# Reordering the first stage of a two-layer trunk kernel: weight units, token load, filler products and row spreading

## What is computed

```python
mod_all = einsum('bd,lde->lbe', silu(c), w_mod) + b_mod      # w_mod: (2, 1024, 6*1024)
shift1, scale1, gate1, shift2, scale2, gate2 = split(mod_all[i], 6)
h = rms_norm(x, norm_g[i, 0]) * (1 + scale1) + shift1
y = pool_mixer(h, pool_w, pool_scale)        # window means, then a 256x256 product per group
x = x + gate1 * rms_norm(y, norm_g[i, 1])
h = rms_norm(x, norm_g[i, 2]) * (1 + scale2) + shift2
y = swiglu(h, ffn_w_gu, ffn_w_down)
```

## Time and profile before

| what | us |
|---|---|
| median of 3 runs | 1280.43 (1277.85 to 1281.45) |
| profiled execution, its own time | 1280.07 |
| its span, first to last instruction | 1278.2 |
| first product of the FFN in it | 70.39 after the span's start |

### The profile page before, as it was taken

One profiled execution on the slowest core, in us unless ns is written; L12 is line 12 of the kernel. 1 busy time (PEld: TensorE's weight loads), 2 busy tenths in 40 slices (PEclk: granted clock), 3 DMA queues, 4 the chain that ended last, 5 costly groups with the idle time before them and its releaser, 6 DMA issues.

```text
span 1278.2 us, 31266 instructions
## 1 busy us (share of the span) xinstructions
PE 1249.0 (98%) x14625; PEld 779.1 (61%) x14625; DVE 387.3 (30%) x591; ACT 214.7 (17%) x320; POOL 109.8 (9%) x134
## 2 busy tenths in 40 slices
PE   6799999999999999999999999999999999999997
PEld 3589999989774354545455454554545545454555
DVE  1567778979872110101101011010101201011012
ACT  3253333474842000000000000000000000000001
POOL 4220000010030000020010010002001000200100
PEclk9899999999999999999999999999999999999999
DMA  9998998959379999999999999999999999999980
GB/s 371 414 358 295 334 333 305 364 197 395 123 245 420 425 423 425 424 402 424 424 407 424 424 409 411 424 409 404 423 421 396 422 424 412 404 424 415 399 355 36
DMA packets 114055, 477.47 MB, mean 374 GB/s; under 512 B 10944, under 2 KB 37280, under 8 KB 113792
## 3 DMA queue, kind: packets, MB, share of 16 engines
q1 hardware_dynamic: 106112, 457.29, 89.1%
q0 software_dynamic: 7664, 17.87, 4.6%
q10 hardware_dynamic: 144, 0.26, 0.1%
HBM read 465.79 MB, written 11.16 MB: 373 GB/s over the span
## 4 chain that ended last, share of the span: by engine, by line
PE 95%; DVE 2%; ACT 1%; POOL 1%; DMA 1%; issue 1%; SPq 0%; DVEq 0%; ACTq 0%
PE ps L2421 23%; PE ps L2407 23%; PE ps L2396 23%; PE ps L1927 7%; PE ps L1928 7%; PE ps L1929 7%; PE ps L1952 1%; PE ps L2014 1%; PE ps L1911 1%; DMA raw<-w_mod 1%; DVE wlo L1572 1%; PE ps L2205 1%; PE ps L1975 0%; PE ps L2035 0%; PE ps L2350 0%
## 5 line engine op out<-in xcount | busy, mean ns | idle before, releaser
L1799 DVE TENSOR_TENSOR act_in<-act_in,ps 128x1344 f32<-128x1344 f32 x16 | 24.9, 1555 | 527.1 <-PE ps L2407 527.1
L1927 PE MATMUL ps<-thi,whi 128*128 128x256 f32 x480 | 136.0, 283 | 0.8 <-DVE wlo L1421 0.8
L1928 PE MATMUL ps<-tlo,whi 128*128 128x256 f32 x480 | 135.8, 283 | 0.0
L1929 PE MATMUL ps<-thi,wlo 128*128 128x256 f32 x480 | 135.8, 283 | 0.0
L2396 PE MATMUL ps<-raw,turned_in 128*32 128x448 f32 x1296 | 123.7, 539 | 0.0
L2407 PE MATMUL ps<-ring_w,turned_in 128*32 128x448 f32 x1248 | 120.6, 539 | 0.0
L2421 PE MATMUL ps<-ring_w,turned_act 128*32 128x256 f32 x2016 | 117.2, 379 | 0.0
L2421 PE MATMUL ps<-raw,turned_act 128*32 128x256 f32 x2016 | 115.5, 379 | 0.0
L1220 ACT ACTIVATE act_in<-ps 128x1344 f32<-128x1344 f32 x16 | 20.7, 1292 | 548.6 <-PE ps L2396 548.6
L1290 DVE TENSOR_TENSOR wlo<-raw,whi 128x2048 fp32r<-128x2048 f32 x41 | 92.9, 2289 | 32.7 <-ACT whi L901 32.7
L2421 PEld LDWEIGHTS ps<-raw,turned_act 128*32 128x32 f32 x2016 | 82.4, 110 | 33.5 <-issue 3.5
(11 more groups left out here) (324 smaller groups left out, 1332.0 us busy)
## 6 DMA issues: line engine op xcount, KB each, us to landing
raw<-moe_w_gu SPq DMA_DIRECT2D x96, 896.0 KB, 12.9
ring_w<-moe_w_gu SPq DMA_DIRECT2D x96, 896.0 KB, 13.0
raw<-w_mod SPq DMA_DIRECT2D x84, 512.0 KB, 5.7
rows<-moe_w_gu SPq DMA_DIRECT2D x48, 896.0 KB
raw<-moe_w_down SPq DMA_DIRECT2D x48, 896.0 KB, 13.9
ring_w<-moe_w_down SPq DMA_DIRECT2D x48, 896.0 KB, 13.4
raw<-ffn_w_gu SPq DMA_DIRECT2D x44, 512.0 KB, 5.6
rows<-moe_w_down SPq DMA_DIRECT2D x24, 896.0 KB
```

What stands on the lines that cost most here:

```text
L1799: dve.tensor_tensor(act_3, act_3, gate_up_ps(1), ALU.mult).then_inc(e_act, 1)
L1927: pe.matmul(out, a_hi, b_hi, start=start, stop=False, skip_group_check=check)
L1928: pe.matmul(out, a_hi, b_lo, start=False, stop=False, skip_group_check=check)
L1929: return pe.matmul(out, a_lo, b_hi, start=False, stop=stop, skip_group_check=check)
```

## The change

It touches the first stage alone:

- **Order of units.** `HEAD` is now group by group: 1, 0, 2, 4, 3. The four shift1 units come ahead of all gate1 units; before, the two groups were interleaved. SP loads in this order, DVE takes all four gate units after the edge columns (before: two ahead of them and two behind), PE's list follows.
- **Tokens first.** `x` (1 MB) is loaded ahead of unit 0; before, it was loaded behind unit 1.
- **Zero products.** 85 at the begin, 8 before the pooled product, 20 before the second mixing product, 20 after each of the first three gate units, 12, 12 and 16 between the waits for the residual, and 20 behind each of units 16, 17 and 18. The tile of zeros is now cleared by DVE.
- **Rows spread with 128 rows of contraction.** The two rows are loaded into row 0 of two tiles of zeros that DVE clears first, so that the product by ones has 128 rows of contraction. POOL waits for the clearing before it issues these loads.
- **PE's order.** The pooled product comes ahead of the spread and of units 2 and 3; units 12 to 15 are spread over the waits, unit 15 behind `turn(0)`.

The core of the diff:

```diff
-HEAD = [(1, 0), (1, 1), (1, 2), (1, 3), (0, 0), (0, 1), (2, 0), (0, 2), (2, 1), (0, 3), (2, 2), (2, 3),
-        (4, 0), (4, 1), (4, 2), (4, 3), (3, 0), (3, 1), (3, 2), (3, 3)]
+HEAD = [(g, pair) for g in (1, 0, 2, 4, 3) for pair in range(4)]
...
+            sp.dma_start(xs[:, :, :], x[0].rearrange("(t p) d -> p t d", p=P)).then_inc(x_loaded, 16)
             for r, (g, pair) in enumerate(HEAD):
                 load(r, 0, mod_unit(0, g, pair))
...
+            for row in wide_rows:
+                dve.memset(row, 0.0).then_inc(padded, 1)
...
-            gate_unit(0)
-            gate_unit(1)
             dve.wait_ge(col_ps, 2)
...
-            gate_unit(2)
-            gate_unit(3)
+            for pair in range(4):
+                gate_unit(pair)
             finish_rows(0, (2,))
...
-                    mm = pe.matmul(bank(b + h), ones[0:1, :], wide_src[:, i * D + h * 512:i * D + h * 512 + 512], start=True, stop=True)
+                    mm = pe.matmul(bank(b + h), ones, wide_rows[i][:, h * 512:h * 512 + 512], start=True, stop=True)
...
+            pe.wait_ge(zeros_ready, 1)
+            keep_clock(4, 85)
+            pe.wait_ge(silu_ready, 1)
+            head_units((0,))
...
+            head_units((1,))
+            keep_clock(4, 8)
...
+            for b in range(4):
+                pooled(b)
+            head_units((2,))
+            pe.wait_ge(wide_loaded, 32)
+            spread(0, 2)
+            head_units((3,))
+            turn_columns(1)
+            pe.wait_ge(wide_ready, 1)
+            spread(1, 2)
+            pe.wait_ge(col_ready, 1)
...
-            head_units((7, 9))
+            head_units((6, 7))
             turn_columns(0)
+            pe.wait_ge(wide_ready, 2)
+            keep_clock(3, 20)
             pe.wait_ge(pooled_done, KC)
             mix(MIX_ORDER[1])
-            pe.wait_ge(wide_ready, 2)
+            for pair in range(1, 4):
+                pe.wait_ge(gate_done, pair)
+                keep_clock(3, 20)
             pe.wait_ge(gate_done, 4)
             row_sum(0, 2)
...
-            head_units(range(12, 16))
+            pe.wait_ge(col_ready, 2)
+            head_units((12,))
+            pe.wait_ge(row_done, done_rank(0, 2))
+            keep_clock(3, 12)
+            pe.wait_ge(gated, 1)
+            head_units((13,))
+            pe.wait_ge(x_done, 1)
+            keep_clock(3, 12)
             pe.wait_ge(gated, T)
+            head_units((14,))
+            keep_clock(3, 16)
             turn(0)
+            head_units((15,))
             turn_columns(4)
-            head_units(range(16, 17))
             turn(1)
-            head_units(range(17, 20))
+            head_units((16,))
+            keep_clock(3, 20)
+            head_units((17,))
+            keep_clock(3, 20)
+            head_units((18,))
+            keep_clock(3, 20)
+            head_units((19,))
             turn_columns(3)
```

More of the change, by code:

```diff
@@ L124 @@
 ROW_ORDER = [[2, 5], [3, 2, 4, 5]]
-ROW_BANK = [[None, None, 0, None, None, 2], [None, None, 0, 2, 6, 6]]
+ROW_BANK = [[None, None, 2, None, None, 2], [None, None, 0, 2, 6, 6]]
 ROW_GAIN = {2: 1, 4: 2, 5: 3}
@@ L336, in build_trunk @@
         hv3 = hv.rearrange("p (k s) -> p k s", k=KC)
-        wide_src = tmp[0:1, 0:2 * D]
+        wide_rows = [rows[:, 6, :], gain[:, 1, :]]
         qk_t = scr[:, 0:4096].rearrange("p (m s) -> p m s", m=2 * NH)
@@ L439, in build_trunk @@
         m1_ps = sem("m1_ps")
+        padded = sem("padded")
         pooled_done = sem("pooled_done")
@@ L730, in _ @@
             pool.memset(rows[:, 5, :], 0.0).then_inc(rows_zeroed, 1)
-            pool.memset(zeros[:, :], 0.0).then_inc(zeros_ready, 1)
             pool.wait_ge(rows_zeroed, 2)
@@ L935, in _ @@
             act.activation(silu_c[:, :], silu_c[:, :], ACT.Silu).then_inc(silu_ready, 1)
-            act.wait_ge(cols_ps, 1)
-            act.copy(cols[:, :, :], ps[:, 6, 0:9 * KC].rearrange("p (i k) -> p i k", k=KC)).then_inc(cols_ready, 1)
-            act.wait_ge(dist_ps, 1)
-            act.activation(bias_row[:, 0:S], ps[0:NH, 5, 0:S], ACT.Copy, scale=HD ** 0.5).then_inc(dist_ready, 1)
             def copy_wide(i, b, dst):
@@ L949, in _ @@
                 square_x(0, t)
-            copy_wide(0, 2, rows[:, 6, :])
+            act.wait_ge(cols_ps, 1)
+            act.copy(cols[:, :, :], ps[:, 6, 0:9 * KC].rearrange("p (i k) -> p i k", k=KC)).then_inc(cols_ready, 1)
+            act.wait_ge(dist_ps, 1)
+            act.activation(bias_row[:, 0:S], ps[0:NH, 5, 0:S], ACT.Copy, scale=HD ** 0.5).then_inc(dist_ready, 1)
             for t in range(T):
                 normalize_tile(0, t)
+            copy_wide(0, 2, rows[:, 6, :])
             head_sum(1)
@@ L959, in _ @@
                                    scale=modc[:, 0, k:k + 1]).then_inc(pooled_ready, 1)
-            copy_wide(1, 1, gain[:, 1, :])
+            copy_wide(1, 2, gain[:, 1, :])
             square_mixed(1)
@@ L1379, in scale_columns @@
                 return dve.tensor_tensor(modc[:, 2 * i, :], modc[:, 4, :], cols[:, 6 + i, :], ALU.mult)
+            dve.memset(zeros[:, :], 0.0).then_inc(zeros_ready, 1)
+            for row in wide_rows:
+                dve.memset(row, 0.0).then_inc(padded, 1)
             dve.wait_ge(pool_loaded[0], 16)
@@ L1963, in turn_columns, with pooled @@
                 mm.then_inc(col_ps, 1)
[L1965 to L1971 removed]
             def spread(i, b):
                 for h in range(2):
[L1975 removed]
+                    mm = pe.matmul(bank(b + h), ones, wide_rows[i][:, h * 512:h * 512 + 512], start=True, stop=True)
                 mm.then_inc(wide_ps, 1)
[L1978 to L1993 removed]
+            def pooled(b):
                 for t in range(T):
@@ L2004, in _ @@
                 mm.then_inc(pooled_ps, 1)
-            pe.wait_ge(first_gain_loaded, 16)
-            spread(1, 1)
-            head_units((4, 5))
             def mix(t):
```

56 lines of the change are left out of this document (23 added, 33 removed).

## The result

The changed kernel takes 1285.63 us, median of 5 runs (1283.60 to 1286.45), against 1280.43 of the kernel before (5 runs, 1277.49 to 1281.45). The ratio is 1.0046, 95% interval 1.0029 to 1.0063: slower by 0.3 to 0.6%. Its profiled execution took 1283.60, with a span of 1281.7 and a mean granted clock of 0.996.

A forecast was written before the change was run, and what follows sets the result against it. PE, busy 98%, bounds the kernel, so a shift of the first FFN product shifts the end. Gate units +2.35 and closing stretch +1.2 make +3.5 us on 1280.07: 1283.6, range 1280.8 to 1288.0.

The forecast's parts named there:

- Part 5: First transpose to last unit: 11.2 us, 1.2 more; clock saves 3.6, unit 15 with copy 1.4 and zeros 3.4 cost.
- the first rival: Slower: clock falls despite zeros, ahead of the row sum and in the closing stretch; +1.8 to +5.8 us; chance 0.39.
- Part 1: Start, tokens first, to the end of the pooled product: it ends at 20.0, where before it was 29.2.
- The bound and the yardstick: PE is busy 98%, so whatever moves the first FFN product, at 70.39, moves the end by as much.
- Part 2: Pooled product's end to the first gate unit: scale fold, copies, mixing product, units 6 and 7; 18.1 us, starting at 38.1.
- E: The time at which the pooled product ends, taken as 20.0, with bounds 18.0 and 21.5.
- Part 3: Gate units on DVE: all four behind the edge columns take 10.5 us, ending at 48.6, 2.35 later than before.
- Part 4: Last gate unit to the first transpose, row sum to second normalization: unchanged at 10.9 us.
- rival 3: Same, smaller loss: the clock set free at the begin stays, pooled product ends at 18.0; 1281.7 us, chance 0.17.

The follow-up runs named there:

- experiment 5: Changed kernel with more zero products in its waits (36 instead of 20 behind each of the first three gate units, more in later waits): 1284.57 us.
- experiment 7: Kernel before plus 60 zero products in one wait, behind units 12 to 15 and ahead of the first transpose: 1277.22 us.
- experiment 8: Kernel before plus zero products in two waits, 20 ahead of the second mixing product and 60 behind units 12 to 15: 1276.90 us.
- experiment 3: Kernel before with the token load ahead of unit 0, nothing else: 1282.19 us.
- experiment 9: Experiment 6 with 36 instead of 20 zero products behind each of the first three gate units, gates still in the new order: 1279.25 us.
- experiment 10: Experiment 6 with the old order of units and gate units, and the zero products fitted to the waits of that order: 1275.97 us.
- experiment 1: Changed kernel without the three blocks of 20 zero products behind units 16, 17 and 18: 1281.41 us.
- experiment 6: Experiment 1 with unit 15 set ahead of the first transpose, turn(0), instead of behind it: 1280.19 us.
- experiment 2: Changed kernel with the old order of units and the old place of the gate units on DVE, zero products as in the change: 1285.04 us.
- experiment 4: Changed kernel without any first-stage zero products except the old 24 ahead of the FFN: 1286.40 us.

## Why the prediction was right

The forecast was 1283.6 with the first FFN product at 73.9. The profiled execution took 1283.60 with 73.97. The median came out 2 us higher, in the range, and on the slower side of 0.3%; the prediction had given that side and "no change" the same chance, 0.48 each. The mechanism held part by part; that the sum fits to 0.1 us is luck, as Part 5 says, and the 2 us of the median are put together from the first rival (up to 1.4) and a later end of Part 1 (about 1).

**The bound and the yardstick** held: the shift at the first FFN product, 3.58, is the shift at the end, 3.53.

**Part 1.** End of the pooled product 19.9, forecast 20.0. ACT had normalized the tokens at 13.98 (14.3 forecast), unit 1 ended at 15.01 at half clock, as the upper of the two values had it, and the pooled product's first pieces ran at 0.50 until 16.2. The 85 zeros cost nothing, as said. Its spread over the traces, 19.9 to 21.0, is within the bounds; that it is worth about 1 us of the median is put together in experiment 5, not measured.

**Part 2.** First gate unit at 37.62, forecast 38.1 (E + 17.7 and not + 18.1). The scale column was ready at 26.36, E + 6.5 (forecast E + 6.4). ACT's eight copies took 3.03 and not 3.5: the term was 0.5 too large. The VectorE operation with two SBUF inputs took 1.07 us here; it began 1.3 us behind the start of POOL's fold (24.00) and ended with the fold's first pass; alone it takes 0.17. Other traces have the same meeting at other moments: it took 1.77 before, 1.55 in experiment 7, 2.35 in experiment 8 (begun with the fold) and 1.01 in experiment 3 (begun in the second pass), and each time it ended within 0.04 us of the end of the pass in which it began, if a pass is half of the fold's 4.66.
The rule quoted from the Trainium skill (SBUF — State Buffer, "Who interferes with whom") fits all five; no kernel was run that takes the meeting apart.

**Part 3.** The four gate units took 10.52, forecast 10.5, and ended at 48.14, forecast 48.6: +1.90 against before, not +2.35, the 0.45 inherited from Part 2. What the new order costs at the end is shown by experiments 9 and 10, 3.3 us by medians and 2.6 by traces; against the kernel before it is less, because that kernel's own gate end (46.24) was late by 0.7, with edge columns at 39.86 against 39.19.

**Part 4.** 48.14 to 58.89 is 10.75, forecast 10.9.

**Part 5** is the term that was mis-sized. From the first transpose to the end of unit 19 the trace has 58.89 to 70.69, 11.8, forecast 11.2; before 9.98. The zeros were taken at 3.4 and cost 4.1 (experiment 1), since the row they were priced from has 24 of them in one block, and three blocks between other products also slow what stands around them; in one block 60 take 3.35. Unit 15 was taken at 1.4 and cost 1.2 (experiment 6). The saving by the clock, 3.6, is 3.3 in experiment 7. The error of +0.6 here and that of -0.45 in Part 2 cancel, with 0.15 of Part 4: the sum came out as +3.58 against +3.5 by luck in its last digits.

Two slips have no weight in it. The row sum's 1.81, set beside the spread's 1.98, is from the chain and not from PE's timeline, which has 1.95; after the change both take 1.98, so the wider contraction did cost nothing. And rival 3 less 1 us is 1280.7, not 1280.8.

**The first rival** happened too, and in part. The prediction made it one case beside the forecast; the runs show both in one kernel. Its mechanism, place and price were right: blocks of zeros with pauses between them lost the clock ahead of the row sum, the price was 1.4 of the 1.8 us given for it (experiments 1 and 5; of the changed kernel's own runs above 1285 there is no trace). What it added, a closing stretch that begins at half clock, did not come: in experiment 1 the clock was back at 51.8.
Beside it stood what the Trainium skill says (TensorE: Matmul & The Clock Gate, Part 1), that the point of change differs from run to run; the two groups of experiment 1 agree with it (0.997 with 1279.4 to 1279.7, 0.994 with 1281.3 to 1282.5).
What the prediction missed in it is what this does to a median: where most runs lose and one keeps, the forecast time is that of the luckiest run.

**The third rival** (E = 18.0) came in no trace. **That the change is right in one part** was in no rival: up to 5.0 us won by zeros in waits were there to be seen as a kernel of its own, and experiments 7, 8 and 10 took them.

## What to carry to other kernels

Price filler products by where they stand: in a wait they cost nothing and were worth up to 5.0 us here; between instructions that are ready they cost their full length, and more when they are broken into blocks (4.1 us for three of 20, 3.35 for one of 60). Their number must fit the shortest wait, or they end up on the path (experiment 2). Where they left a pause at the end of a wait, the clock was lost in some traces (experiments 1 and 8) and kept in others (the changed kernel, experiment 7). An earlier start of one product is worth what the next join lets through: the pooled product came 9 us earlier, and with all that goes with it gave 0.9. Work moved out of an engine's idle time costs its length less what its move sets free: two gate units of 2.6 us each, and 2.95 at the end of the gates. And look at how the runs are spread before a median is explained by one trace.

## What the runs showed of the hardware

- TensorE's granted clock differed between runs of the same program, and the times fell into groups 2 us apart by it (experiment 1: 0.997, and 0.993 to 0.994; experiment 8: 0.997 to 0.998, and 0.994 to 0.996). In experiment 7 the two groups meet at 0.995, and in the kernel before the mean clock doesn't tell its two groups apart.
- With 1.29 us of zeros in each 2.64 us the clock was kept in the changed kernel's trace and lost in those of experiments 1 and 6; with 6.42 of 6.88 us (experiment 5) it was kept, and the times of all four runs agreed within 0.35 us.
- A pause of 1.76 us behind 3.5 us of zeros was followed by half clock 2 us later in experiment 8, while 1.35 us at the same place in experiment 7 was not. One execution each.
- Units of 16 products took 0.915 us each in a row of four and 1.00 each between blocks of zeros. 60 zero products in one block took 3.35 us (experiment 2), one of 20 between units 1.22.
- A VectorE operation with two SBUF inputs, 0.17 us alone, took 1.01 to 2.35 us beside a GpSimd operation that reads SBUF, and ended with a pass of it in five traces.
- In experiment 4, unit 0 took 1.94 us, the length of half clock, in a stretch where the granted clock is written as 1.00, as in the kernel before (1.93); with zeros ahead of it, it took 1.07. The record of the clock in that trace has its first change at 38.9 and says nothing of the time before it.
